# Unread products of ones in TensorE's waits at the opening and at two norms

## The chip, the cores and the metric

One Trainium2 chip, one of its cores. The metric is the device time of one execution in microseconds (us). Three runs of the kernel before took 3430.41, 3430.74 and 3436.06 us, a median of 3430.74 us. TensorE's clock has two levels here, 1.2 and 2.4 GHz; the profile shows the granted clock as a share of the higher.

## The reference, cut to what matters

Two decoder blocks for 256 tokens of width 2048, in float32. The first block normalises the tokens and a memory of 256 rows, projects both, runs three kinds of attention, merges them and ends in a gated feed-forward part. The second block has a modulated norm, an attention and a recurrent branch, and then a second modulated norm ahead of a product-key expert layer. The norm is the same each time:

```
def _rmsnorm(x, g):
    xf = x.astype(jnp.float32)
    y = xf * lax.rsqrt(jnp.mean(xf * xf, axis=-1, keepdims=True) + EPS)
    return y.astype(x.dtype) * g
...
h = _rmsnorm(x, g_mix[l]) * (1.0 + sc1[:, None, :]) + sh1[:, None, :]
mix = _hybrid_mixer(h, ...)                     # first product: h @ w_in
x = x + ga1[:, None, :] * mix
h = _rmsnorm(x, g_ffn[l]) * (1.0 + sc2[:, None, :]) + sh2[:, None, :]
x = x + ga2[:, None, :] * _peer(h, ...)         # first product: h @ w_q
```

The kernel's very first product is the memory's: `mkv = rms_norm(mem, g_mem[layer]) @ w_mem_kv[layer]`.

## The kernel before, in words

Weights come from DRAM in pieces of 1 MB (128 partitions x 2048). Four pieces, in the slots s = 0 to 3 of `raw`, `hi` and `lo`, make a quad, which is one product of 256 tokens with a 2048 x 512 slice of weights. ScalarE rounds a piece into `hi` (`round_piece`, line 560), VectorE or GpSimd subtracts it from `raw` into `lo` (`rest_piece`, line 1067 or 410), and TensorE adds three matmuls for each 128 x 512 tile: hi by the leading part of the activations, lo by the leading part, hi by their rest (`split_products`, lines 1898 to 1900). `wide_piece` is one piece: 4 tiles x 2 halves of the tokens x 3 = 24 matmuls of 128x512 (fp32r). A quad is 96 of them. Slots are released from engine to engine by semaphores (`hi_done`, `lo_done`, `piece_used`), so that loading, rounding and subtracting run at the rate at which TensorE finishes pieces.

Activations must stand transposed for this. `turn` (line 1928) transposes 8 blocks of 128x128 into a pair of PSUM banks; VectorE multiplies by the gain (and adds the shift) into `fold` (lines 1115, 1113 or 1131), ScalarE rounds that into `hTh` or `memTh` (line 598), VectorE writes the rest to `hTl` or `memTl` (line 1075). Four such groups, g = 0 to 3, make all 2048 columns. `norm_turn` (line 1937) waits for the group's source and turns it; `fold_turn` puts it in banks 4 and 5 or 6 and 7 by turns.

A norm stage of the second block is `normed_quad` (line 1944), called at line 2270 ahead of the input projection (source u = 3) and at line 2348 ahead of the query projection (u = 4). Its TensorE program is: turn groups 0, 1 and 2, then wide_piece 0, turn group 3, wide_pieces 1 to 3. Ahead of it stand the last products of the step before, whose sum must be added to `x` by VectorE (line 1409, or 1612 and 1614), squared by ScalarE (line 570), turned to a reciprocal root by both, and applied by ScalarE (line 583, `xn`) before group 0 can be turned. ScalarE's program makes groups 0 and 1 of `xn` first, and makes group 2 only when group 0 has been folded and rounded.

At the opening, TensorE waits for the identity and then turns groups 0 and 1 of the memory (lines 1962 and 1963), does wide_piece 0 with the memory's transposes, turns groups 2 and 3, and goes on with pieces 1 to 3. VectorE's program there is: fill `ones` (line 1124), write `onesr` (line 1125, which signals `onesr_in`), wait for the constants `cols`, fold group 0, rest of piece 0, rest of memTl 0, fold group 1, and so on. SyncE's queue has issued identity, memory and first pieces by then; its next load waits for the first `lo`.

`ones` is a 128x128 float32 tile. Before the change its one reader on TensorE is line 2297 (`lru_squares`), a float32 product 256 columns wide. Other float32 products, 128x128 each, are those of `key_scores` (line 2340): 4 x 2 = 8 in a call.

Of the kernel before, what the change touches and what calls it, by code (L numbers as in the profile page):

```python
# [12 lines left out]
P = 128  # L13
# [155 lines left out]
def program(nc, t):  # L169
# [4 lines left out]
    def at(name, shape, dt, off):  # L174
        return nc.alloc_sbuf_tensor_at(name, shape, dt, offset=base0 + off)
# [105 lines left out]
    ones = at("ones", [P, P], F32, CO + 1 * K)  # L281
# [32 lines left out]
    ps = nc.alloc_psum_tensor("ps", [P, 8, 512], F32)  # L314
# [10 lines left out]
    def fold_bank(f):  # L325
        if FOLD_ATT <= f < FOLD_LRU:
            return 6
        return 4 if FOLD_M <= f < FOLD_FFN else 4 + 2 * (f % 2)
# [11 lines left out]
    def sem(name):  # L340

        if name not in sems:
            assert name in SIGNALS, name
            sems[name] = nc.alloc_semaphore(name)
        return sems[name]
# [6 lines left out]
    with nc.Block() as block:  # L352
# [1540 lines left out]
        def _(pe):  # L1893
            T = nc.tensor
# [7 lines left out]
            def wide_piece(q, s, b, th=None, tl=None):  # L1902

                th, tl = (hTh, hTl) if th is None else (th, tl)
                pe.wait_ge(lo_done, 4 * q + (s + 1))
                for k in range(4):
                    for m in range(TOK):
                        ins = split_products(ps[:, b + m, :], th, tl,
                                             (slice(None), 4 * s + k, slice(P * m, P * m + P)), s,
                                             slice(512 * k, 512 * k + 512), s == 0 and k == 0, s == 3 and k == 3)  # L1910
                ins.then_inc(piece_used, 1)
# [12 lines left out]
            def turn(b, tiles):  # L1924

                for k in range(4):
                    for m in range(TOK):
                        ins = T.transpose(quarters(b)[:, k, P * m:P * m + P], tiles(k, m), ident[:])  # L1928
                return ins

            def fold_turn(f, tiles):
                free = f if FOLD_M <= f < FOLD_FFN else f - 1
                if free >= 1:
                    pe.wait_ge(sem("fold_t"), free)
                turn(fold_bank(f), tiles).then_inc(sem("fold_tr"), 1)

            def norm_turn(f0, g, src, u):
                if u == 0:
                    pe.wait_ge(sem(f"mem_in{g}"), 16)
                else:  # L1940
                    pe.wait_ge(sem("xn_done"), 8 * max(u - 2, 0) + 2 * g + 2)
                fold_turn(f0 + g, lambda k, m: src[:, m, P * (4 * g + k):P * (4 * g + k) + P])

            def normed_quad(f0, src, u, q, b):

                for g in range(3):
                    norm_turn(f0, g, src, u)
                for s in range(4):
                    pe.wait_ge(sem("fold_lo"), f0 + s + 1)
                    wide_piece(q, s, b)  # L1950
                    if s == 0:
                        norm_turn(f0, 3, src, u)

            pe.wait_ge(sem("ident_in"), 16)

            def bias_by_distance(s):
                if s == 3:
                    pe.wait_ge(sem("const_in"), 16 * 10)
                    pe.wait_ge(sem("fold_t"), FOLD_X)
                    T.matmul(ps[0:6, 7, :], tabs[:], oneh[:], start=True, stop=True).then_inc(sem("bias_mm"), 1)  # L1960

            norm_turn(FOLD_MEM, 0, memraw, 0)
            norm_turn(FOLD_MEM, 1, memraw, 0)
            for s in range(4):
                pe.wait_ge(sem("fold_lo"), FOLD_MEM + s + 1)
                wide_piece(0, s, 0, memTh, memTl)
                if s == 0:
                    norm_turn(FOLD_MEM, 2, memraw, 0)
                    norm_turn(FOLD_MEM, 3, memraw, 0)
                bias_by_distance(s)  # L1970
# [295 lines left out]
            for c in range(IN_CHUNKS):  # L2266
                if c >= 2:
                    pe.wait_ge(sem("in_out"), c - 1)
                if c == 0:
                    normed_quad(FOLD_MIX2, xn, 3, Q_IN2, 0)  # L2270
                    continue
                for s in range(4):
                    i = 4 * (c - 3) + s
                    wide_piece(Q_IN2 + c, s, 2 * (c % 2))
                    if s == (1 if c == 9 else 0) and c - 1 in TURNED:
                        in_turn(c - 1)
                    if (c, s) == (1, 0):
                        forget_logits()
                    if i in OUTPUT_AT:
                        output2(OUTPUT_AT[i])  # L2280
                    if i in TURN_AT:
                        turn2(TURN_AT[i])
                    if i in SCORES_AT:
                        scores2(SCORES_AT[i])
                    if c == 8:
                        lru_products(2 * s)
                        lru_products(2 * s + 1)
                    if c == 9 and s in (0, 2):
                        attention_turn(s // 2)
# [54 lines left out]
            for c in range(4):  # L2344
                if c >= 2:
                    pe.wait_ge(sem("pq_out"), c - 1)
                if c == 0:
                    normed_quad(FOLD_PEER, xn, 4, Q_PQ, 0)
                else:
                    for s in range(4):  # L2350
                        wide_piece(Q_PQ + c, s, 2 * (c % 2))
                if c >= 1:
                    pq_turn(c - 1)
                if c >= 2:
                    key_scores(c - 2)
# [218 lines left out]
```

## Time and profile before

| | |
|---|---|
| median of three runs | 3430.74 us (3430.41 to 3436.06) |
| the profiled execution | 3430.05 us, of it span 3428.1 us |
| mean granted TensorE clock | 0.996 |
| PE busy | 3376.2 us, 98% |
| PEld, DVE, ACT, POOL busy | 82%, 66%, 41%, 18% |
| DMA | 797.53 MB, mean 233 GB/s |

PE is TensorE's matmuls and PEld its weight loads, which run beside them; DVE is VectorE, ACT ScalarE, POOL GpSimd, SP SyncE. Durations of single matmuls overlap, so the rate of a row of them is read from the distance of their starts, not from the durations. A float32 matmul that isn't a transpose has two records for each product.

### The profile page before, as it was taken

The numbers are of one execution on the slowest core, as the hardware profiler recorded it, in microseconds if no ns is written. First come the engines' busy times: TensorE is split into PE (matmuls) and PEld (weight loads), VectorE is DVE, ScalarE is ACT, GpSimd is POOL, SyncE is SP. The second block draws the span as 40 slices with busy tenths as digits, with TensorE's granted clock in tenths as the row PEclk, the third lists the DMA queues.
The fourth block names the chain that finished last, engine by engine and source line by source line (L and its number), as shares of the span: only waits on it lengthen the run. The fifth ranks groups of instructions, "written<-read, shape, count | busy, mean of one in ns | idle before, by whom it ended". The sixth has DMA issues, their size and how long they took to land.

```text
span 3428.1 us, 42144 instructions
## 1 busy us (share of the span) xinstructions
PE 3376.2 (98%) x15504; PEld 2796.2 (82%) x15504; DVE 2272.0 (66%) x2268; ACT 1409.9 (41%) x1123; POOL 626.6 (18%) x333
## 2 busy tenths in 40 slices
PE   8999999999999999989998999999999999999998
PEld 7888888888888888878887888888888888888886
DVE  7664545788887888755566494555557777765556
ACT  6333343443343333443454344444443333333333
POOL 0000003300000000100000188777730000000000
PEclk9999999999999999999999999999999999999999
DMA  7555556888887888744454456677676666656552
GB/s 261 196 189 183 190 196 237 312 313 317 319 324 290 315 324 312 255 154 162 158 196 172 172 209 218 236 249 243 237 282 234 222 234 232 233 200 229 197 206 100
DMA packets 151236, 797.53 MB, mean 233 GB/s; under 512 B 15084, under 2 KB 48124, under 8 KB 63960
## 3 DMA queue, kind: packets, MB, share of 16 engines
q1 hardware_dynamic: 85168, 610.47, 48.8%
q0 software_dynamic: 26992, 149.99, 11.8%
q10 hardware_dynamic: 38976, 35.66, 3.3%
q8 instruction: 72, 1.18, 0.1%
q14 instruction: 28, 0.23, 0.0%
HBM read 756.15 MB, written 39.91 MB: 232 GB/s over the span
## 4 chain that ended last, share of the span: by engine, by line
PE 93%; DVE 3%; ACT 1%; issue 1%; DMA 1%; POOL 0%; SPq 0%; DVEq 0%; ACTq 0%; POOLq 0%
PE ps L1898 29%; PE ps L1900 29%; PE ps L1899 29%; PE ps L1928 2%; DMA adaraw<-in_w_ada 1%; PE ps L2400 1%; DVE adaacc L1335 1%; ACT hi L560 1%; DVE lo L1067 0%; PE ps L2030 0%; PE ps L2007 0%; PE ps L2221 0%; PE ps L2018 0%; PE ps L2340 0%; DMA cols<-in_cols 0%
## 5 line engine op out<-in xcount | busy, mean ns | idle before, releaser
L560 ACT CAST hi<-raw 128x2048 fp32r<-128x2048 f32 x576 | 1100.3, 1911 | 1782.7 <-PE ps L1900 1767.0
L1067 DVE TENSOR_TENSOR lo<-raw,hi 128x2048 fp32r<-128x2048 f32 x468 | 1071.2, 2291 | 656.5 <-ACT hi L560 644.4
L1898 PE MATMUL ps<-hi,hTh 128*128 128x512 f32 x3040 | 1197.8, 394 | 0.7 <-DVE hTl L1075 0.7
L1899 PE MATMUL ps<-lo,hTh 128*128 128x512 f32 x3040 | 1185.1, 390 | 0.0
L1900 PE MATMUL ps<-hi,hTl 128*128 128x512 f32 x3040 | 1185.0, 390 | 0.0
L1900 PEld LDWEIGHTS ps<-hi,hTl 128*128 128x128 f32 x3040 | 571.1, 188 | 120.6
L1898 PEld LDWEIGHTS ps<-hi,hTh 128*128 128x128 f32 x3040 | 571.8, 188 | 116.2 <-DVE hTl L1075 1.1
L1899 PEld LDWEIGHTS ps<-lo,hTh 128*128 128x128 f32 x3040 | 572.0, 188 | 113.7
L410 POOL TENSOR_TENSOR lo<-raw,hi 128x2048 fp32r<-128x2048 f32 x108 | 500.2, 4634 | 230.5 <-ACT hi L560 230.5
L1898 PE MATMUL ps<-hi,pactTh 128*128 128x512 f32 x992 | 388.2, 391 | 0.0
L1900 PE MATMUL ps<-hi,pactTl 128*128 128x512 f32 x992 | 386.3, 389 | 0.0
L1899 PE MATMUL ps<-lo,pactTh 128*128 128x512 f32 x992 | 386.0, 389 | 0.0
L1777 DVE TENSOR_TENSOR y<-y,ps 128x1024 f32<-128x1024 f32 x124 | 151.3, 1220 | 133.7 <-PE ps L1900 133.2
L1335 DVE SCALAR_TENSOR_TENSOR adaacc<-adaraw,cs,adaacc 128x1024 f32<-128x1024 f32 x180 | 230.6, 1281 | 9.0 <-DMA adaraw<-in_w_ada 5.6
L1900 PEld LDWEIGHTS ps<-hi,pactTl 128*128 128x128 f32 x992 | 186.2, 188 | 38.9
L1899 PEld LDWEIGHTS ps<-lo,pactTh 128*128 128x128 f32 x992 | 186.3, 188 | 38.0
L1898 PEld LDWEIGHTS ps<-hi,pactTh 128*128 128x128 f32 x992 | 186.2, 188 | 37.8
L458 POOL DMA_DIRECT2D adaraw<-in_w_ada x96 | 51.1, 533 | 713.8 <-DVEq L1339 709.8
L1745 DVE TENSOR_TENSOR wst<-wst,ps 128x512 f32<-128x512 f32 x64 | 44.0, 687 | 166.0 <-ACT wst L967 166.0
L1898 PE MATMUL ps<-hi,factTh 128*128 128x512 f32 x320 | 124.8, 390 | 0.8 <-DVE x L1409 0.6
L1900 PE MATMUL ps<-hi,factTl 128*128 128x512 f32 x320 | 124.5, 389 | 0.0
L1899 PE MATMUL ps<-lo,factTh 128*128 128x512 f32 x320 | 124.5, 389 | 0.0
(372 smaller groups left out, 2405.0 us busy)
## 6 DMA issues: line engine op xcount, KB each, us to landing
raw<-in_w_peer SPq DMA_DIRECT2D x256, 1024.0 KB, 4.8
raw<-in_w_ffn SPq DMA_DIRECT2D x132, 1024.0 KB, 6.2
adaraw<-in_w_ada POOLq DMA_DIRECT2D x96, 1024.0 KB, 6.3
raw<-in_w_first SPq DMA_DIRECT2D x88, 1024.0 KB, 4.8
raw<-in_w_second SPq DMA_DIRECT2D x72, 1024.0 KB, 4.8
raw<-in_w_merge SPq DMA_DIRECT2D x28, 1024.0 KB, 6.5
w_scratch<-wst ACTq DMA_DIRECT2D x64, 256.0 KB, 3.7
wc<-w_scratch POOLq DMA_DIRECT2D x32, 512.0 KB, 5.0
```

The costliest lines, as they stand in the source:

```text
L410: nc.gpsimd.tensor_tensor(lo[:, s, :], raw[:, s, :], hi[:, s, :].bitcast(F32), ALU.subtract)\
L458: pool.dma_start(adaraw[:, j % 2, :, :].rearrange("p k n -> p (k n)"), t["w_ada"][8 * a + j])\
L560: nc.scalar.copy(hi[:, s, :], raw[:, s, :]).then_inc(hi_done, 1)
L1067: V.tensor_tensor(lo[:, s, :], raw[:, s, :], hi[:, s, :].bitcast(F32), ALU.subtract).then_inc(lo_done, 1)
L1335: ins = V.scalar_tensor_tensor(acc, src, col, acc, ALU.mult, ALU.add)
L1745: V.tensor_tensor(wst[:, v], wst[:, v], weight_parts[:, :, 1], ALU.add).then_inc(sem("w_sum"), 1)
L1777: V.tensor_tensor(yc, yc, pair(6 if s % 2 == 0 else 2), ALU.add).then_inc(sem("y_sum"), 1)
L1898: T.matmul(out, th[stat], hi[:, s, cut], start=start, stop=False)
L1899: T.matmul(out, th[stat], lo[:, s, cut], start=False, stop=False)
L1900: return T.matmul(out, tl[stat], hi[:, s, cut], start=False, stop=stop)
L1928: ins = T.transpose(quarters(b)[:, k, P * m:P * m + P], tiles(k, m), ident[:])
L2400: ins = T.matmul(ps[:, 4 + k // 2, SEQ * (k % 2):SEQ * (k % 2) + SEQ], oh1[:, v, k], oh2[:, v, k].rearrange("p e b -> p (e b)"), start=Tru ...
```

## The change

TensorE gets a helper that issues n products of `ones` by `ones`, 128 columns wide, into the first quarter of PSUM bank 2. Nothing reads them, and they signal nothing. They stand in five places: 24 at the start, behind a new wait for `onesr_in` and ahead of the wait for the identity; 24 between the memory's groups 0 and 1; 22 behind group 1; and in `normed_quad`, which runs twice, 36 ahead of group 0 and 22 behind group 1.

```diff
+            def kept_running(n):
+
+                for _ in range(n):
+                    T.matmul(ps[:, 2, 0:P], ones[:], ones[:], start=True, stop=True)
...
             def normed_quad(f0, src, u, q, b):
 
+                kept_running(36)
                 for g in range(3):
                     norm_turn(f0, g, src, u)
+                    if g == 1:
+                        kept_running(22)
                 for s in range(4):
...
+            pe.wait_ge(sem("onesr_in"), 1)
+            kept_running(24)
             pe.wait_ge(sem("ident_in"), 16)
...
             norm_turn(FOLD_MEM, 0, memraw, 0)
+            kept_running(24)
             norm_turn(FOLD_MEM, 1, memraw, 0)
+            kept_running(22)
             for s in range(4):
```

## Rows read from the trace of the kernel before

**Rows 1.** The page's part 4: the chain that ended last, by engine.

```profile
PE 93%; DVE 3%; ACT 1%; issue 1%; DMA 1%; POOL 0%; SPq 0%; DVEq 0%; ACTq 0%; POOLq 0%
```

**Rows 2.** Waits of PE: line, awaited; us in total, times, longest.

```profile
PE ps L1928 <- ACT xn L583: 16.7, 4, 6.2
PE ps L1928 <- DMA memraw<-in_mem: 8.9, 2, 6.7
```

**Rows 3.** Timeline, opening: start us, us, engine, line, operation, count, idle before.

```profile
1.29 0.15 DVE L1125 CAST onesr<-ones 128x1 fp32r<-128x1 f32 x1
6.73 1.94 PE L1928 MATMUL ps<-ident,memraw 128*128 128x128 f32 x8 [6.73 <-DMA memraw<-in_mem]
9.47 1.66 DVE L1131 TENSOR_SCALAR fold<-ps,cols 128x256 f32<-128x256 f32 x4 [8.03 <-DMA cols<-in_cols]
10.84 1.97 PE L1928 MATMUL ps<-ident,memraw 128*128 128x128 f32 x8 [2.16 <-DMA memraw<-in_mem]
14.60 0.80 PE L1898 MATMUL ps<-hi,memTh 128*128 128x512 f32 x1 [1.79 <-DVE memTl L1075]
...
20.31 0.49 PE L1899 MATMUL ps<-lo,memTh 128*128 128x512 f32 x1
...
20.87 0.39 PE L1898 MATMUL ps<-hi,memTh 128*128 128x512 f32 x1
...
22.93 1.91 PE L1928 MATMUL ps<-ident,memraw 128*128 128x128 f32 x16
```

**Rows 4.** Timeline, TensorE in a call of the key scores.

```profile
1925.49 1.04 PE L1928 MATMUL ps<-ident,stage 128*128 128x128 f32 x8
1926.36 1.95 PE L2340 MATMUL ps<-keysT,pqT 128*128 128x128 f32 x16
1928.07 0.47 PE L1898 MATMUL ps<-hi,hTh 128*128 128x512 f32 x1
```

**Rows 5.** Timeline, the other products with ones, 256 columns.

```profile
1763.39 1.99 PE L2297 MATMUL ps<-lsq,ones 128*128 128x256 f32 x8 [0.84 <-DVE lsq L1599]
```

**Rows 6.** Timeline, the first normed quad.

```profile
1459.63 0.39 PE L1900 MATMUL ps<-hi,lastTl 128*128 128x512 f32 x1
...
1464.90 3.34 PE L1928 MATMUL ps<-ident,xn 128*128 128x128 f32 x16 [4.88 <-ACT xn L583]
...
1466.97 3.71 DVE L1115 TENSOR_SCALAR fold<-ps,gmod,modT 128x256 f32<-128x256 f32 x8 [3.42 <-PE ps L1928]
...
1471.24 1.97 PE L1928 MATMUL ps<-ident,xn 128*128 128x128 f32 x8 [2.99 <-ACT xn L583]
...
1472.86 0.77 PE L1898 MATMUL ps<-hi,hTh 128*128 128x512 f32 x1
...
1474.28 0.55 PE L1898 MATMUL ps<-hi,hTh 128*128 128x512 f32 x1
...
1479.26 1.03 PE L1928 MATMUL ps<-ident,xn 128*128 128x128 f32 x8
```

**Rows 7.** Timeline, the second normed quad.

```profile
1842.91 0.39 PE L1900 MATMUL ps<-hi,hTl 128*128 128x512 f32 x1
1849.52 3.68 PE L1928 MATMUL ps<-ident,xn 128*128 128x128 f32 x16 [6.22 <-ACT xn L583]
...
1855.85 1.09 PE L1928 MATMUL ps<-ident,xn 128*128 128x128 f32 x8 [2.66 <-ACT xn L583]
...
1860.11 0.48 PE L1900 MATMUL ps<-hi,hTl 128*128 128x512 f32 x1
...
1863.86 1.04 PE L1928 MATMUL ps<-ident,xn 128*128 128x128 f32 x8
```

**Rows 8.** Windows: the stretch, busy us of PE, PEld, DVE, ACT, POOL, PEclk, DMA share, GB/s.

```profile
1459.90:1464.90 5.00, 0.12 (x1) 0.00 (x0) 1.79 (x5) 2.92 (x8) 0.00 (x0) 0.94 0.56 210
1464.90:1468.30 3.40, 3.34 (x16) 3.10 (x16) 1.33 (x3) 2.96 (x3) 0.00 (x0) 0.58 0.00 0
1849.50:1853.20 3.70, 3.68 (x16) 3.28 (x16) 1.61 (x4) 2.98 (x3) 0.00 (x0) 0.50 0.00 0
```

**Rows 9.** DMA: queue of instruction fetches (packets, MB, share); then one load of the opening.

```profile
q8 instruction: 72, 1.18, 0.1%
...
cols<-in_cols SPq DMA_DIRECT2D x1, 90.5 KB, 7.0
```

## The prediction

> **What bounds the kernel now.** I read the chain that ended last first: 93% of it is PE [rows 1]. So a microsecond that TensorE loses anywhere is nearly always a microsecond of the total, and the change lives in the little that is left. PE's waits say where that is: 16.7 us behind `xn` in four waits, and 8.9 us behind the memory's loads in two [rows 2]. These are the two normed quads and the opening. Then the timelines: how long is each gap, and at which level do the matmuls after it run? A wide matmul follows the next after (22.93 - 20.87) / 9 = 0.228 us at the opening's end, but 14.60 to 20.31 us holds 13 of them, 0.44 us each [rows 3]; after the norms fewer of them are so far apart. A group of 8 transposes takes 0.87 us in a busy stretch [rows 4]; after the gaps of 4.88 and 6.22 us, 16 take 3.34 and 3.68 us, with a granted clock of 0.58 and 0.50 [rows 6 to 8], that is mostly or wholly the 1.2 GHz level. (The granted clock isn't of use at the opening; the distance of the matmuls is.)
>
> So there is something to win: the matmuls and transposes behind the gaps at 2.4 GHz. The price is that TensorE's program is in order, and a product that isn't done when the awaited data comes holds them up. The whole case is whether 24 + 24 + 22 and 36 + 22 products fit the gaps.
>
> **What one product costs.** The nearest row is `key_scores`: float32, 128x128 by 128x128, 8 products, 16 records, 1926.36 to 1928.07 us, so 1.71 / 8 = 0.214 us each at the higher level [rows 4]. The tile of ones itself is read in a product twice as wide: 4 products in about 2 us [rows 5], which is the same rate for twice the columns. Lower bound: a product costs one record of the two, 0.107 us, as it would if repeated weights or an unread output made it cheaper. Upper bound: 0.427 us, twice the 0.214 us, at the lower level, as the wide matmuls (0.44 against 0.228) are near twice as slow there. I take 0.214, and 0.427 where the array is still at the lower level.
>
> The Trainium skill has a rule that would make this another change: "TensorE: Matmul & The Clock Gate", section "Back-to-back issue gap", gives about 81 ns for a matmul 128 columns wide in a stream of load-and-multiply pairs, and a planner who takes that for a product finds all of them hidden. The row says 214 ns, and it decides. By 81 ns the sum would be that of the first rival below.
>
> **The opening.** `onesr` is written at 1.44 us [rows 3], and the first 24 products start at about 1.5 us, from the lower level. How long that lasts isn't in the trace for these products. After TensorE's work began again it ran at the lower level from 14.60 to 20.31 (5.7 us), from 1471.24 to 1474.28 (3.0) and from 1855.85 to 1860.11 (4.3) [rows 3, 6, 7]. I take 4.3 and keep 3.0 and 5.7: each microsecond at the lower level costs half of one, so
> - 24 products: 24 x 0.214 + 4.3 / 2 = 7.3 us, to 8.8 us (8.1 to 9.5). The memory's group 0, which started at 6.73 us, starts 2.1 us late. It is turned in 0.87 us, to 9.7. VectorE couldn't fold it before 9.47 in any case, for `cols` [rows 3], so its chain slips by only some 0.6 us; SyncE's next load, which waits for the first `lo`, as well, and nothing is short of that load.
> - 24 products at 0.214: 5.1 us, to 14.8. Group 1 had its data by 10.84: 4.0 us late. Turned by 15.7.
> - 22 products: 4.7 us, to 20.4. Only now does the first wide piece start, which had been held by memTl until 14.60 [rows 3]. memTl 0 is ready by some 15.2, and VectorE's fold of group 1 moves from 14.5 to about 16.0, still in time for piece 1. What is late is TensorE's own queue.
> - The piece takes 24 x 0.228 = 5.5 us and ends at 25.9. Before, it ended at 22.93, with 13 matmuls at 0.44 us in it.
>
> So the opening loses 2.9 us (2.3 to 3.6): 5.8 us of late start, 2.9 us back from the clock.
>
> **The first normed quad.** The last product of the step before starts at 1459.63 and the next could at 1459.86 [rows 6]. 36 x 0.214 = 7.7 us, to 1467.6, where `xn` was there at 1464.90: 2.7 us late. Turned at the higher level, the last of 8 ends 1.04 us after the first starts [rows 4] and not 1.98 us [the fold starts at 1466.97, rows 6], so the fold starts at about 1468.7, 1.7 us late, and with it ScalarE's group 2 of `xn`: from 1471.24 to about 1473.0. TensorE: groups 0 and 1 turned, 1.74 us, to 1469.3; 22 products, 4.7 us, to 1474.0. Again the queue is 1 us later than the data. Group 2 is turned by 1474.9 (before: 1472.86), the piece with 5.5 us ends at 1480.35. Before: 1479.26. A loss of 1.1 us.
>
> **The second.** The same, with a longer gap: 1843.14 + 7.7 = 1850.8 instead of 1849.52 (1.3 late), groups 0 and 1 to 1852.6, 22 products to 1857.3, where `xn` group 2 would be there at about 1856.2; turned by 1858.2, the piece ends at 1863.6. Before: 1863.86 [rows 7]. A gain of 0.2 us, as here nine wide matmuls had run at the lower level.
>
> Behind each place TensorE goes on without a wait, with pieces that are rounded and subtracted at its own rate, so what it has lost or won stays. Nothing else is added: 70 + 2 x 58 = 186 products, 372 records. Their writes to bank 2 meet no reader, as the folds read banks 4 to 7.
>
> **Sum.** 2.9 + 1.1 - 0.2 = 3.8 us. On the profiled execution's 3430.05 us that is 3433.8; that run lies 0.7 us under the median, on whose scale the forecast is 3434.5 us. Its own range: 0.6 us either way for the opening's clock, 0.5 for the norms, and the runs of before scatter by more on the high side: 3432 to 3437.5.
>
> **Rivals.**
> 1. A product costs 0.107 us and all of them fit. Then 24 of them at the lower level end at 6.6 us, under 6.73; 24 end at 10.2, under 10.84; 22 end at 14.1, under 14.60; the piece ends at 20.1 instead of 22.93: 2.9 us won. First norm: 36 end at 1463.7, transposes start on time and end 0.94 us earlier, group 2 starts at 1470.3, the piece ends at 1476.6: 2.6 won. Second: 2.6 won by the same steps. 8.1 us in all, 3422.6 us. For it: the counts would fit the gaps almost to the tenth. Against it: 16 records for 8 products and 1.71 us [rows 4], and the same rate with ones [rows 5]. 12%.
> 2. TensorE must wait for its own instructions, once, at the opening, where the added products ask for four instructions each 0.214 us, more than twice the rate of wide matmuls (two in 0.228), while the loads have the DMA engines full. Price: what a small load took there, 7.0 us [rows 9], so 3441.5. It decides from 3.1 us on, which is what is left between my 3.8 us and 0.2% of the total. For it: TensorE starts at 1.5 and not at 6.7 us. Against it: `key_scores` runs at the same rate without a gap, and only 72 fetches of 16 KB serve the whole span [rows 9]. 8%.
> 3. The products of ones don't raise or hold the clock, the change doesn't do what it says. The opening is then 70 x 0.427 + 16 x 0.21 = 33.3 us from 1.5, to 34.8 instead of 14.60: 20 us lost. At the first norm the clock falls inside the 36 as it fell in the gap (a mean of 0.94 over 5.0 us [rows 8] puts that near 1464.3): 20 products at 0.214, 16 at 0.427, 16 transposes at 0.21, 22 products at 0.427 and 8 transposes end near 1485.4 instead of 1472.86, 12.5 us lost; about as much at the second. 3476 us. Against it: no row has a busy TensorE going down. 4%.
>
> **How the numbers follow.** My case has 76%. The range goes down to the first rival's 3422 and up to 3440, which leaves out most of the second and the third. A measurement here can tell 0.2%, 6.9 us, from no change: the first rival is faster by more (12%), the second and third slower by more and my case's upper tail with them (14%), my case is within (74%).
>
> **What would show it.** After the change: a group `ps<-ones` with 372 records; the first wide matmul at 20.4 us (14.1 to 14.6 by the first rival); the wide matmuls behind all three places at 0.228 us from the first; the transposes of `xn` 16 in some 1.9 us at a clock of 1.0; no wait of PE for `memraw` or `xn`, as it comes to each of them late; group 0 of the first norm turned 2.7 us and the wide piece finished 1.1 us later after the last product of the step before than now, at the second norm 1.3 us later and 0.2 us earlier. I am wrong if PE still waits at these places, which would mean that a product is cheaper than 0.214 us, or if the wide matmuls there still stand 0.43 us apart.

## The result, and the profile after

The changed kernel took 3437.01 us (median of 20 runs, 3433.86 to 3442.11) against 3432.24 us for the kernel before, measured beside it (20 runs, 3429.52 to 3437.43). The ratio is 1.0013, with a 95% interval of 1.0007 to 1.0019, so it is slower by 4.5 us (2.4 to 6.5). Forecast were 3.8 us more, and 3434.5 us. Of the 2.5 us between 3434.5 and 3437.01, 1.5 are the baseline, whose median over 20 runs lies that much above the one of the three runs shown ahead; 1.0 is the change. The prediction held that 0.2% is the least that can be told from no change; with 20 runs of each kernel the interval is 0.06% to either side, so that these 0.13% can be told, though they are less than 0.2%.

The profiled execution has a span of 3435.8 us. Its page's part 1 (busy us, share of the span, records) shows TensorE 32 us busier with 372 more records, while the span grew by 7.7 us:

```profile
PE 3408.6 (99%) x15876; PEld 2832.5 (82%) x15876; DVE 2270.6 (66%) x2268; ACT 1410.5 (41%) x1123; POOL 626.2 (18%) x333
```

The timeline of TensorE at the opening, which answers to [rows 3] (start us, duration, engine, line, operation, records, idle before and what ended it):

```profile
1.50 7.71 PE L1940 MATMUL ps<-ones 128*128 128x128 f32 x48 [1.50 <-DVE onesr L1125]
9.05 1.04 PE L1928 MATMUL ps<-ident,memraw 128*128 128x128 f32 x8
9.92 5.52 PE L1940 MATMUL ps<-ones 128*128 128x128 f32 x48
15.28 1.04 PE L1928 MATMUL ps<-ident,memraw 128*128 128x128 f32 x8
16.16 5.08 PE L1940 MATMUL ps<-ones 128*128 128x128 f32 x44
20.99 0.47 PE L1898 MATMUL ps<-hi,memTh 128*128 128x512 f32 x1
21.30 0.39 PE L1899 MATMUL ps<-lo,memTh 128*128 128x512 f32 x1
...
26.55 1.91 PE L1928 MATMUL ps<-ident,memraw 128*128 128x128 f32 x16
```

There is no idle time left, and that is the trouble: each row starts where the one above it lets go, never where its data came. The first wide matmul starts at 20.99 us instead of 14.60, and group 2 is turned at 26.55 instead of 22.93. In return the wide matmuls behind the first stand 0.23 us apart, which is the higher level.

The same at the first normed quad [rows 6]:

```profile
1461.92 0.39 PE L1900 MATMUL ps<-hi,lastTl 128*128 128x512 f32 x1
1462.15 8.20 PE L1940 MATMUL ps<-ones 128*128 128x128 f32 x72
1470.19 1.91 PE L1928 MATMUL ps<-ident,xn 128*128 128x128 f32 x16
1471.93 5.08 PE L1940 MATMUL ps<-ones 128*128 128x128 f32 x44
1476.85 1.04 PE L1928 MATMUL ps<-ident,xn 128*128 128x128 f32 x8
1477.64 0.48 PE L1898 MATMUL ps<-hi,hTh 128*128 128x512 f32 x1
...
1483.18 1.04 PE L1928 MATMUL ps<-ident,xn 128*128 128x128 f32 x8
```

and at the second [rows 7]:

```profile
1846.68 0.39 PE L1900 MATMUL ps<-hi,hTl 128*128 128x512 f32 x1
1846.90 8.20 PE L1940 MATMUL ps<-ones 128*128 128x128 f32 x72
...
1861.60 1.04 PE L1928 MATMUL ps<-ident,xn 128*128 128x128 f32 x8
...
1867.94 1.04 PE L1928 MATMUL ps<-ident,xn 128*128 128x128 f32 x8
```

The windows of the two norms (the stretch, busy us of PE with its records, PEclk, DMA share, GB/s) have no idle time either and a clock that stays up [rows 8]:

```profile
1462.20:1477.60 15.40, 15.40 (x140) 1.00 0.19 69
1846.90:1862.40 15.50, 15.50 (x142) 1.00 0.19 69
```

From here on a place is measured by one distance: at the opening the start of group 2's transposes, at a norm the time from the start of the last product of the step before to the start of group 3's transposes (1459.63 to 1479.26 is 19.63 us before, 1461.92 to 1483.18 is 21.26 us after). These distances don't hang on when TensorE came to the place. They are of one execution each. The last two columns are of all runs: the median less the kernel before's that was measured beside it, and the ratio of the two.

| kernel | opening | norm 1 | norm 2 | median less the kernel before's | ratio (95%) |
|---|---|---|---|---|---|
| before | 22.93 | 19.63 | 20.95 | | |
| the change | 26.55 | 21.26 | 21.26 | +4.8 | 1.0013 (1.0007 to 1.0019) |
| e1 opening only | 25.90 | 20.45 | 21.97 | +4.3 | 1.0016 (1.0007 to 1.0025) |
| e2 norms only | 21.40 | 21.26 | 21.26 | +2.1 | 1.0006 (0.9997 to 1.0015) |
| e3 fitted counts | 20.00 | 17.36 | 18.70 | -4.0 | 0.9990 (0.9981 to 0.9999) |
| e4 one record | 27.82 | 17.14 | 19.36 | +3.8 | 1.0008 (0.9999 to 1.0017) |
| e9 the same again | 20.75 | 17.15 | 19.35 | one execution | |
| e5 wide ones | 19.86 | 17.43 | 18.77 | -7.6 | 0.9978 (0.9969 to 0.9988) |
| e6 first waits only | 22.98 | 18.74 | 20.01 | -3.3 | 0.9990 (0.9980 to 1.0000) |
| e7 later waits only | 21.75 | 18.57 | 21.01 | -0.5 | 0.9997 (0.9988 to 1.0007) |
| e8 refitted | 19.92 | 17.13 | 18.47 | -6.1 | 0.9980 (0.9971 to 0.9989) |
| e10 wide, refitted | 19.89 | 17.23 | 18.55 | -6.7 | 0.9981 (0.9972 to 0.9990) |

### The profile page after: what moved, and what is told of

It reads as the page before. It is cut to its first block, busy times and chain, and to the rows that moved or that the text cites. A ratio compares the mean times of both kernels' runs of the same rounds, so it can differ in the third digit from the quotient of the medians.

```text
span 3435.8 us, 42888 instructions
## 1 busy us (share of the span) xinstructions
PE 3408.6 (99%) x15876; PEld 2832.5 (82%) x15876; DVE 2270.6 (66%) x2268; ACT 1410.5 (41%) x1123; POOL 626.2 (18%) x333
## 4 chain that ended last, share of the span: by engine, by line
PE 95%; DVE 2%; DMA 1%; ACT 1%; issue 1%; POOL 0%; ACTq 0%; DVEq 0%; POOLq 0%
PE ps L1898 29%; PE ps L1900 29%; PE ps L1899 29%; PE ps L1928 2%; PE ps L1940 1%; PE ps L2412 1%; DMA w_scratch<-wst 1%; ACT hi L560 1%; DMA adaraw<-in_w_ada 0%; PE ps L2042 0%; PE ps L2019 0%; DVE lo L1067 0%; PE ps L2233 0%; DVE adaacc L1335 0%; PE ps L2030 0%
```

## The experiments

All are edits of the changed kernel. A record is one line of the trace for one matmul; "won" and "lost" at a place compare its distance with the kernel before's row of the table. In e4, e5, e9 and e10 the transposes stand on line 1930, the wide products on 1900 to 1902 and the unread ones on 1942.

**e1 and e2: which place loses.** e1 takes the products out of `normed_quad`, e2 those of the opening with their wait:

```diff
-                kept_running(36)
...
-                    if g == 1:
-                        kept_running(22)
```

```diff
-            pe.wait_ge(sem("onesr_in"), 1)
-            kept_running(24)
...
             norm_turn(FOLD_MEM, 0, memraw, 0)
-            kept_running(24)
             norm_turn(FOLD_MEM, 1, memraw, 0)
-            kept_running(22)
```

> Only the opening's 24 + 24 + 22 products stand; normed_quad is as before. Theory (a product costs 0.223 us, as the changed kernel's trace shows, and TensorE's own queue sets the end of each place): the transposes of the memory's group 2 start at 26.5 us instead of 22.93, and the total is 3.6 us over the kernel before, ratio 1.001. Rival (the loss comes from the norms, and the opening's shift is taken back later, as the shift fell by 1.3 us between 725 and 1443 us in the profiled execution): under 2.3 us over.

> Only the 36 + 22 products of the two normed quads stand; the opening is as before. Theory: the first quad's group 3 is turned 21.26 us after the last product of the step before (19.63 before, 1.6 lost), the second's 21.26 after (20.95 before, 0.3 lost), total 1.9 us over the kernel before. Rival (the norms lose nothing, what is lost there was scatter of one execution): no more than 0.5 us over.

Measured: e1 5.5 us slower by its ratio (2.4 to 8.6), its group 2 turned 3.0 us later than before; e2 2.1 us slower (-1.0 to 5.1), its norms 1.6 and 0.3 us longer. The opening loses, and e1's rival (under 2.3 us) lies just outside its interval. For the norms nothing is decided: e2's interval takes in both its theory and its rival, and its trace decides only as far as one execution of the kernel before can be trusted. e1 has the norms of the kernel before, and yet they differ from that kernel's:

```profile
1467.58 3.67 PE L1928 MATMUL ps<-ident,xn 128*128 128x128 f32 x16 [4.88 <-ACT xn L583]
...
1482.76 1.03 PE L1928 MATMUL ps<-ident,xn 128*128 128x128 f32 x8
```

The wait is the same 4.88 us, but 16 transposes take 3.67 us and not 3.34, eight wide matmuls follow 0.43 us apart and not four, and the norm is 0.8 us longer. At the second norm e1 takes 21.97 us, 1.0 more than the kernel before. In e2, seven wide matmuls stand so far apart at the opening where the kernel before had 13, and group 2 is turned 1.5 us earlier, of which 0.3 are a wide piece that could start earlier. So the moment at which the clock falls and rises differs from one execution to the next, by 0.8 to 1.3 us at a place, with the same code. A loss read from one pair of traces is no better than that: against e1's norms, those of e2 lose 0.8 us and win 0.7, which is nothing in the sum.

**e3: counts that fit.**

```diff
-                kept_running(36)
+                kept_running(21)
...
-                        kept_running(22)
+                        kept_running(16)
...
-            kept_running(24)
+            kept_running(13)
...
             norm_turn(FOLD_MEM, 0, memraw, 0)
-            kept_running(24)
+            kept_running(13)
             norm_turn(FOLD_MEM, 1, memraw, 0)
-            kept_running(22)
+            kept_running(12)
```

> The same places with counts that fit the gaps at 0.223 us a product: 13, 13 and 12 at the opening, 21 and 16 in normed_quad. Theory: every product is done before the awaited data, the transposes and wide matmuls behind run at the higher level, and each place wins what the clock had cost: 2.9 us at the opening, 2.6 and 2.6 at the norms, 8.1 us in all, ratio 0.9976. Rival 1 (fewer products don't lift or hold the clock, as less of the gap is filled): the gaps are as before and the gain is under 3 us. Rival 2 (products cost something else than time in the queue, such as a wait for instructions): no gain, or a loss.

Its opening and the start of its first norm:

```profile
1.50 5.85 PE L1940 MATMUL ps<-ones 128*128 128x128 f32 x26 [1.50 <-DVE onesr L1125]
7.19 1.04 PE L1928 MATMUL ps<-ident,memraw 128*128 128x128 f32 x8
8.06 3.07 PE L1940 MATMUL ps<-ones 128*128 128x128 f32 x26
...
14.44 0.48 PE L1898 MATMUL ps<-hi,memTh 128*128 128x512 f32 x1
...
1460.06 4.85 PE L1940 MATMUL ps<-ones 128*128 128x128 f32 x42
1465.10 2.32 PE L1928 MATMUL ps<-ident,xn 128*128 128x128 f32 x16 [0.20 <-ACT xn L583]
```

The wide piece starts at 14.44 us, and TensorE is idle for 0.20 us before `xn`: it is ready just before its data. The places win 2.9, 2.3 and 2.3 us, 7.5 against 8.1 expected, which neither rival allows; the clock can be had with 112 products instead of 186. The median won only 4.0 us (0.3 to 6.5), so the ratio that the theory gave, 0.9976, fell. That is taken up with e8.

**e4 and e9: one record for each product.** The counts of the change, but a tile in fp32r:

```diff
+    rounded = at("rounded", [P, P], F32R, CO + 5 * K)
+            V.tensor_copy(rounded[:], ones[:])
-                    T.matmul(ps[:, 2, 0:P], ones[:], ones[:], start=True, stop=True)
+                    T.matmul(ps[:, 2, 0:P], rounded[:], rounded[:], start=True, stop=True)
```

> The counts of the change, but the products read a rounded (fp32r) tile of ones, which VectorE writes at the opening in one more copy of about 0.2 us, so that each product has one record and not two. Theory (the loss is the length of the float32 product and nothing else): a product takes 0.11 us, 24 and 22 of them 2.6 and 2.4 us, 36 of them 4.0 us, all fit, and 8 us are won as in the fitted kernel, ratio 0.9976. Rival 1 (a product of 128 columns in fp32r takes as long as in float32): 0.22 us each, and 5 us lost as by the change. Rival 2 (unread products disturb otherwise): fits by the queue but wins nothing.

> The one-record kernel once more, unchanged, for a second trace of its opening. In the first, 70 products of 128 columns in fp32r and 16 transposes kept TensorE busy from 1.64 to 19.87 us, and the wide matmuls behind still stood 0.43 us apart. Theory (these products don't raise the clock at the opening, in any execution): the same again, wide matmuls 0.43 us apart, group 2 turned near 27.8 us. Rival (it was one execution's chance, as this kernel's times scatter over 13 us): the level rises before the wide piece, which starts by 15 us with its matmuls 0.23 us apart.

The opening of e4, and the transposes of its second norm:

```profile
1.64 5.38 PE L1942 MATMUL ps<-rounded 128*128 128x128 f32 x24 [1.64 <-DVE onesr L1127]
6.82 1.93 PE L1930 MATMUL ps<-ident,memraw 128*128 128x128 f32 x8
8.40 5.36 PE L1942 MATMUL ps<-rounded 128*128 128x128 f32 x24
13.56 1.93 PE L1930 MATMUL ps<-ident,memraw 128*128 128x128 f32 x8
15.14 4.93 PE L1942 MATMUL ps<-rounded 128*128 128x128 f32 x22
19.87 0.73 PE L1900 MATMUL ps<-hi,memTh 128*128 128x512 f32 x1
...
1854.98 3.41 PE L1930 MATMUL ps<-ident,xn 128*128 128x128 f32 x16 [2.25 <-ACT xn L584]
```

and of e9, the same program in a second execution:

```profile
1.63 5.38 PE L1942 MATMUL ps<-rounded 128*128 128x128 f32 x24 [1.63 <-DVE onesr L1127]
...
8.39 3.71 PE L1942 MATMUL ps<-rounded 128*128 128x128 f32 x24
11.93 1.06 PE L1930 MATMUL ps<-ident,memraw 128*128 128x128 f32 x8
12.75 2.65 PE L1942 MATMUL ps<-rounded 128*128 128x128 f32 x22
15.24 0.45 PE L1900 MATMUL ps<-hi,memTh 128*128 128x512 f32 x1
```

My expectation of e4 fell. A product does take half: 36 in 4.13 us at the norms, where both traces win 2.5 and 1.6 us. (At the second norm the products leave 2.25 us of the wait open, the level falls in it, and the transposes behind take 3.41 and 3.31 us.) But at the opening it took 0.22 us, since the level stayed low: in e4 TensorE worked without a gap from 1.64 to 19.87 us, and the wide matmuls behind still stood 0.43 us apart, twelve of them. Neither theory nor rivals had this; my third rival of the prediction, at 4%, is what happened, for these products only. e9 says that it was that execution's: there the level rose in the second group of products (24 in 3.54 us), at about 10.2 us. The times of e4's kernel range from 3427.55 to 3440.46 us, 13 us where those of the other changed kernels have 3 to 10, which fits an opening of either kind.

The level is read from distances here, as the granted clock is 1.00 in all of the opening's rows of every trace but e6's. e6 shows that the distances do mean the lower level: its clock had risen and fallen once by then, and the granted clock is 0.50 where its wide matmuls stand 0.43 us apart (the stretch, busy us of PE with its records, PEclk, DMA share, GB/s):

```profile
14.60:20.00 5.40, 5.30 (x13) 0.50 1.02 417
```

With float32 products at the start the level was up after 3.1 us (e1), 4.4 (the change), 5.3 (e6), 5.6 (e3) and about 5.8 (e8); in e3 and e8 all of the first group ran at the lower level, and in e8 it rose only within the eight transposes behind:

```profile
6.78 1.32 PE L1928 MATMUL ps<-ident,memraw 128*128 128x128 f32 x8
```

The products of 512 columns (e5, e10) had it up after some 2.8 us. So in seven traces of seven the level was up by 7.4 us, in e9 by 10.2 and in e4 not by 19.87. That the narrow single-record products are the unsure ones rests on these two traces, and what it is in them isn't shown. The Trainium skill, "TensorE: Matmul & The Clock Gate", section "Part 4: PE-mode transpose", says that transposes don't bring up the full clock. This case's traces don't bear it out: in e8 the level rises among them, and at the second norm of the kernel before, 16 of them were all that TensorE did ahead of a rise from 0.50 to 1.00 (rows under the third rival below).

**e5: long products.** The fitted counts, 512 columns in fp32r, of the same ones:

```diff
+                    T.matmul(ps[:, 2, :].rearrange("p (o n) -> p o n", o=4), rounded[:],
+                             rounded[:].rearrange("p (o n) -> p o n", o=1).to_broadcast([P, 4, P]),
+                             start=True, stop=True)
```

> As the fitted kernel (13, 13, 12; 21, 16), but each product is 512 columns wide in fp32r and of ones: one record, some 0.227 us at the higher level, so nearly the fitted kernel's time in the queue. Theory (what the one-record kernel lacked at the opening was the length of its products, not other values or another type): the wide matmuls behind the opening stand 0.23 us apart from the first, group 2 there is turned at some 20.0 us, and the three places win 8 us in the trace. Rival (products of ones in fp32r don't raise the clock at the opening, whatever their width): the opening's wide matmuls start 0.43 us apart as in the one-record kernel, and the opening loses.

```profile
1.63 4.57 PE L1942 MATMUL ps<-rounded 128*128 128x512 f32 x13 [1.63 <-DVE onesr L1127]
...
14.28 0.50 PE L1900 MATMUL ps<-hi,memTh 128*128 128x512 f32 x1
14.62 0.39 PE L1901 MATMUL ps<-lo,memTh 128*128 128x512 f32 x1
```

The theory holds: level up at the opening, 3.1, 2.2 and 2.2 us won in the places, and 7.6 us by the median. Neither ones as values nor fp32r keep the clock down.

**e6 and e7: which waits need filling.** e6 has 13 and 21 products ahead of the first transposes and no others; e7 has 13, 12 and 16 behind groups 0 and 1 and none ahead (its wait for `onesr_in` stands behind group 0). Their diffs, e6 first:

```diff
-                kept_running(36)
+                kept_running(21)
...
-                    if g == 1:
-                        kept_running(22)
...
-            kept_running(24)
+            kept_running(13)
...
             norm_turn(FOLD_MEM, 0, memraw, 0)
-            kept_running(24)
             norm_turn(FOLD_MEM, 1, memraw, 0)
-            kept_running(22)
```

```diff
-                kept_running(36)
...
-                        kept_running(22)
+                        kept_running(16)
...
-            pe.wait_ge(sem("onesr_in"), 1)
-            kept_running(24)
...
             norm_turn(FOLD_MEM, 0, memraw, 0)
-            kept_running(24)
+            pe.wait_ge(sem("onesr_in"), 1)
+            kept_running(13)
             norm_turn(FOLD_MEM, 1, memraw, 0)
-            kept_running(22)
+            kept_running(12)
```

> Only the products ahead of the first transposes of each place: 13 at the opening, 21 in normed_quad, none behind groups 0 and 1. Theory (once up, the clock outlives the 2 to 3 us waits that follow, as in the kernel before it outlived 4.4 of the 4.9 us ahead of the first norm): the later products are needless, transposes and wide matmuls run at the higher level all the same, and the places win the fitted kernel's 8 us. Rival (every wait must be filled): the clock falls in the later waits, the first matmuls of each wide piece stand 0.43 us apart, and under 4 us are won.

> Only the later products: 13 and 12 at the opening (behind groups 0 and 1), 16 behind group 1 in normed_quad. Theory (products start at the lower level, where each costs 0.43 us, so that they overrun their wait, and only what is behind them gains): opening 2.0 us late and 2.9 gained, 0.9 won; first norm 2.5 late and 1.5 gained, 1.0 lost; second 2.6 late and 1.7 gained, 0.9 lost; the total is 1 us over the kernel before. Rival (the later products carry the gain): the total is over 3 us under it.

e6, at the opening and at the first norm:

```profile
11.32 1.97 PE L1928 MATMUL ps<-ident,memraw 128*128 128x128 f32 x8 [3.27 <-DMA memraw<-in_mem]
14.70 0.79 PE L1898 MATMUL ps<-hi,memTh 128*128 128x512 f32 x1 [1.41 <-DVE memTl L1075]
...
1470.06 1.09 PE L1928 MATMUL ps<-ident,xn 128*128 128x128 f32 x8 [3.14 <-ACT xn L583]
```

The rival is right. Behind the later wait of 3.27 us the opening is at the lower level again, with 13 wide matmuls 0.43 us apart: nothing is won (22.98 us, against 22.93 in the kernel before and 21.40 in e2). At the first norm eight transposes still run at the higher level behind 3.14 us, and then nine wide matmuls don't: 0.9 us are won each time where 2.3 can be had (at the second norm the eight transposes are slow as well, and three wide matmuls). The places win 1.8 us in all. That the level had outlived most of a 4.9 us wait behind wide matmuls said nothing of a 3.1 us wait behind 16 transposes.

e7:

```profile
8.64 4.24 PE L1940 MATMUL ps<-ones 128*128 128x128 f32 x26
...
1852.18 4.74 PE L1940 MATMUL ps<-ones 128*128 128x128 f32 x32
```

13 products take 4.07 us here (to 12.71) and 16 take 4.58 (to 1856.76), 0.31 and 0.29 each: they start at the lower level and raise it. The opening wins 1.2 us, the first norm 1.1, the second loses 0.1, and the median is 0.5 us under the kernel before, within its interval. The theory's mechanism holds at the opening and the second norm, but not its sum: it had the places lose 1.0 us, and they win 2.2. At the first norm the level was up before the products began, for 16 of them took 3.57 us; all that stood ahead of them behind the 4.88 us wait were 16 transposes. The median doesn't decide: theory (1 us over) and rival (over 3 us under) both lie in its interval, 2.4 us over to 4.1 under. So both kinds of wait have to be filled: the places win 1.8 and 2.2 us with one kind, and 7.5 to 8.0 with both. The medians (3.3 and 0.5 against 4.0 to 7.6) go the same way, but e6's can't be told from e3's.

**e8 and e10: counts for each wait.** e8 in float32: 12, 13, 12 at the opening, 20 at the first norm, 27 at the second, 14 behind group 1. e10 with e5's wide products: 15 behind group 1, else the same.

```diff
-                kept_running(36)
+                kept_running(20 if u == 3 else 27)
```

> The fitted kernel with 12, 13 and 12 at the opening, 20 at the first norm and 27 at the second, 14 behind group 1. Theory (the fitted kernel's places win 8.4 us in its trace, and the 4 us that the rest of that execution lost, in waits for VectorE's x and for the expert weights, is scatter of single executions): again 8 us or more in the places, and a median 6 to 8 us under the kernel before. Rival (a late transfer or VectorE sets later waits and takes half of the gain back whatever the places win): a median 3 to 5 us under it.

> The wide products (512 columns, fp32r) with counts set for each wait: 12, 13 and 12 at the opening, 20 at the first norm and 27 at the second, 15 behind group 1. Theory (all three places are won as in the fitted kernels, and no product is late): 8 to 8.7 us won in the trace, a median 7 to 8 us under the kernel before, ratio 0.9977. Rival (the wide ones' better median than the float32 ones' was scatter, and both stand at 6 us): ratio 0.9982 or more.

The places win 3.0, 2.5 and 2.5 us in e8 and 3.0, 2.4 and 2.4 in e10, and the medians 6.1 and 6.7. (The 8.4 us that e8's expectation gives for the fitted kernel are 7.5 by the distances used here.) e10's ratio, 0.9981, lies between what theory and rival wanted; three kernels at 0.9978, 0.9980 and 0.9981 can't be told apart. They all beat the kernel before and the change.

The medians of e3, e8 and e10 have 4.0, 6.1 and 6.7 us of the 7.5, 8.0 and 7.8 that the places win, e5's has all of its 7.5; of the intervals only e3's leaves the places' sum out. One wait of e8 (line, awaited, us in total, times, longest) shows where single executions lose some:

```profile
PE ps L1928 <- DVE x L1371: 3.1, 1, 3.1
```

This wait, near 657 us, is 1.6 to 1.8 us in seven traces (before, the change, e1, e2, e5, e6, e10) and 3.0 to 3.1 us in five (e3, e4, e7, e8, e9). It doesn't follow TensorE's lead: e5 came there 3.1 us earlier than the kernel before and waited 1.8 us, e4 4.9 us later and waited 3.1. The change's own trace has another:

```profile
PE ps L1928 <- DVE pact L1761: 2.1, 1, 2.1
```

0.2 us in six traces, 0.5 to 2.8 in the others, e2 with 2.3 among them. So a good part of what one execution shows beyond the places is scatter: the change's span grew by 7.7 us, of which the places are 5.6. What sets the two values of the first wait is not shown. Whether a rest of 1 to 2 us of the fitted kernels' gain is always given back stays open; e8's interval, 3.8 to 9.9 us, holds both, and both its theory and its rival.

## Why the prediction was right

**The bound and the order of things.** TensorE's queue sets the end at all three places, as said: no wait for `memraw` or `xn` is left, and the product that comes before the data holds it up. The forecast of the opening was 8.8, 14.8, 20.4 and 25.9 us; measured are 9.05, 15.28, 20.99 and 26.55. The first norm was to lose 1.1 us and lost 1.6; the second to win 0.2 and lost 0.3. Sum 3.8 against 5.6.

**The term that was mis-sized** is the price of a product. I took 1.71 / 8 = 0.214 us from `key_scores`. The trace of the change has 24 in 15.28 - 9.92 = 5.36 us, and 22 in 1476.85 - 1471.93 = 4.92 us: 0.2235 us. 186 products at 0.0095 us more are 1.8 us, the whole of the difference. The products of ones cost what `key_scores` had cost; the row was misread. The same stretch of the kernel before, cut inside the group, so that the count gives each record's start:

```profile
1926.69 1.61 PE L2340 MATMUL ps<-keysT,pqT 128*128 128x128 f32 x13
...
1927.59 0.72 PE L2340 MATMUL ps<-keysT,pqT 128*128 128x128 f32 x5
```

From 13 to 5 records left, 8 records start in 0.90 us: 0.1125 each, 0.225 a product. 15 such steps are 1.68 us, and what was left of the 1.71 us for the step from the last record to the wide matmul is only 0.03 us: I had divided 15 steps by 16. The same holds at the opening, where 22 products ahead of the wide piece took 20.99 - 16.16 = 4.83 us and not 4.92.

**The lower level at the start.** Taken: 4.3 us, between 3.0 and 5.7. 24 products took 7.55 us; at 0.2235 they would take 5.36, and 2.19 us more is 4.4 us at the lower level. In e1 they took 6.89 us, 3.1 us at it. Of the five openings with float32 products four lie within the bounds, and e8's, at about 5.8 us, a little above. That 4.3 met 4.4 so closely is luck, twice. It differs by up to 2.7 us between executions. And the 4.3 is itself misread from [rows 7]: the eight transposes at 1855.85 took 1.09 us and were at the higher level, and only 1856.9 to 1860.2, 3.3 us, were at the lower. With 3.3 the sum would have been 3.3 us instead of 3.8, also inside the measured interval.

**The rivals.** The first (a product is 0.107 us, 3422.6 us) is wrong of float32, and e4 and e9 show what it would have brought even if it were right: its price at the norms, and an opening that goes either way. The rule of the Trainium skill that spoke for it, 81 ns in "Back-to-back issue gap", isn't met by any row here; the shortest is 0.11 us for a record of 128 columns. The second (a wait for instructions) has no trace: 72 fetches became 75, and nothing stands between the products. The third is wrong of the float32 products: a clock of 1.00 at both norms, and wide matmuls 0.23 us apart behind all three places. But what was said against it, that no row has a busy TensorE going down, is not so. The kernel before has one at its second norm (the same columns as above):

```profile
1849.50:1853.20 3.70, 3.68 (x16) 0.50 0.00 0
1854.50:1855.80 1.30, 0.00 (x0) 1.00 0.00 0
1855.90:1856.70 0.80, 0.80 (x8) 1.00 0.00 0
1857.00:1860.10 3.10, 3.10 (x8) 0.50 0.17 32
```

Sixteen transposes run at 0.50, the clock rises in the wait behind them, eight transposes run at 1.00, and then it falls in the midst of wide matmuls. So a clock that is up at the end of a wait isn't safe yet, and 4% was low for a rival that e4 then showed of other products.

The 8.1 us that the first rival's sum gave for filled waits are close to what e8 (8.0), e10 (7.8), e3 and e5 (7.5) win in their places.

**A weak point.** I read the losses against one execution of the kernel before. With e1's norms (20.45 and 21.97) and e2's opening (21.40) averaged in, the change loses 4.1 us at the opening (26.2, with e1's, against 22.2), 1.2 at the first norm and wins 0.2 at the second: 5.1 us, inside the measured 2.4 to 6.5, as 5.6 is. That the norms lose at all is thus not shown; at the opening the change loses against either execution.

## What to carry to other kernels

Work that only keeps TensorE's clock up must end before the awaited data: count its own queue time from the trace, per product and at the level it will run at, and fit the number to each wait; here 112 or 114 products instead of 186 turned a loss of 4.5 us into a gain of 4.0 to 7.6. Fill every wait of a chain, since a wait left open behind a filled one undid it at the opening and took more than half of it at the norms. Products of 512 columns, or float32 ones with their two records, had the level up at the opening in seven traces of seven, the short single-record ones late in one and not at all in the other. When a cadence is read from a group of rows, take it from starts inside the group, as the step to the next kind of instruction can be shorter.

## What the runs showed that was not expected

- TensorE can be busy without a gap for 18.2 us and stay at 1.2 GHz: 70 products of 128 columns in fp32r with 16 transposes between them, 1.64 to 19.87 us in e4. In e9 the same program had risen at about 10.2 us. The 36 + 22 such products at the norms, which start from the higher level or follow the transposes, ended at it both times.
- The level at the end of a wait isn't a function of that wait alone: TensorE was still at 2.4 GHz for eight transposes after 3.14 us of waiting and then fell during work (e6), as in the kernel before at its second norm, and four or eight wide matmuls were affected behind one and the same wait of 4.88 us (before, e1).
- Transposes can be all that stands ahead of a rise to 2.4 GHz: 16 of them in 3.7 us at the second norm of the kernel before, where the granted clock was 1.00 by 1854.5, before TensorE's next instruction at 1855.85, and 16 at the first norm of e7.
